# Gate products stacked in row groups, and the gate-up bias of an expert as four products of 32 rows

## The reference, cut to what matters

```
# in the mixer: a low-rank gate, rank 16, 1024 -> 16 -> 512
glr = xn @ w_in[:, glr columns]                        # 512 x 16
log_decay = log_sigmoid(glr @ gla_gate_up + gla_gate_bias) / 16
# in the experts: for every expert e and its (up to 128) rows
h = xb @ w_gate_up[e] + b_gate_up[e]                   # 128 x 2048
gate, up = min(h[:, ::2], 7), clip(h[:, 1::2], -7, 7)
act = (up + 1) * gate * sigmoid(1.702 * gate)
y = act @ w_down[e] + b_down[e]
```

## Time and profile before

| what | us |
|---|---|
| three runs: median (lowest, highest) | 1867.94 (1866.09, 1868.38) |
| the profiled execution: its own time | 1873.76 |
| span of its records | 1871.8 |
| PE, PEld busy | 1820.0 (97%), 1493.8 (80%) |
| DVE, ACT, POOL busy | 1402.6 (75%), 1112.8 (59%), 131.9 (7%) |
| experts stage, first product to the end | 708.2 to 1871.8 |

### The profile page before, as it was taken

The page is one execution under the profiler, slowest core; times in us unless marked ns, Lnnn a source line. Parts: engine busy times, 40 slices in busy tenths (PEclk is TensorE's granted clock), DMA queues, the critical chain, the costliest instruction groups (busy, mean ns, idle before and its releaser), DMA issues.

```text
span 1871.8 us, 24808 instructions
## 1 busy us (share of the span) xinstructions
PE 1820.0 (97%) x9054; PEld 1493.8 (80%) x9055; DVE 1402.6 (75%) x1294; ACT 1112.8 (59%) x994; POOL 131.9 (7%) x112
## 2 busy tenths in 40 slices
PE   6998999999999997999999999999999999999997
PEld 5776788898888875888888888888888888888885
DVE  3136444426333567999999999999999999999997
ACT  3343322226432254777777777777777777777774
POOL 0000100000000006000000000000000000000001
PEclk9998999999999997999999999999999999999998
DMA  6222042221233386999999999999999999999993
GB/s 210 72 85 67 23 170 90 90 68 36 91 113 121 118 305 228 369 376 369 367 376 365 363 379 368 368 379 368 364 382 367 373 374 368 372 375 372 368 376 127
DMA packets 100038, 493.56 MB, mean 264 GB/s; under 512 B 15434, under 2 KB 17482, under 8 KB 50320
## 3 DMA queue, kind: packets, MB, share of 16 engines
q1 hardware_dynamic: 90080, 475.63, 67.4%
q0 software_dynamic: 9616, 16.62, 3.5%
q10 hardware_dynamic: 288, 0.59, 0.1%
HBM read 484.57 MB, written 24.69 MB: 272 GB/s over the span
## 4 chain that ended last, share of the span: by engine, by line
PE 61%; DVE 1%; ACT 0%; POOL 0%; issue 0%; DVEq 0%; ACTq 0%
PE psum L1782 25%; PE psum L1785 12%; PE psum L1795 12%; PE psum L1800 6%; PE psum L1745 2%; PE psum L1753 1%; PE psum L1775 1%; DVE expert_chunk L1936 0%; DVE h_sb L2101 0%; DVE expert_lo L1626 0%; ACT expert_hi L1621 0%; POOL total_rstd L2019 0%; PE psum L1925 0%; PE psum L1919 0%; DVE gate_values L1865 0%; ACT up_values L2050 0%
## 5 line engine op out<-in xcount | busy, mean ns | idle before, releaser
L1626 DVE TENSOR_TENSOR expert_lo<-expert_chunk,expert_hi 128x2048 fp32r<-128x2048 f32 x384 | 864.5, 2285 | 46.3 <-ACT expert_hi L1621 37.3
L1621 ACT CAST expert_hi<-expert_chunk 128x2048 fp32r<-128x2048 f32 x384 | 735.4, 1917 | 233.7 <-PE psum L1785 201.6
L263 DVE TENSOR_TENSOR chunk_lo<-chunk,chunk_hi 128x2048 fp32r<-128x2048 f32 x48 | 109.9, 2290 | 283.1 <-ACT chunk_hi L259 283.0
L1782 PE MATMUL psum<-expert_hi,rowsT_hi 128*128 128x512 f32 x992 | 273.0, 397 | 0.0
L1782 PE MATMUL psum<-expert_hi,rowsT_lo 128*128 128x512 f32 x992 | 266.6, 391 | 0.0
L1785 PE MATMUL psum<-expert_lo,rowsT_hi 128*128 128x512 f32 x992 | 266.0, 390 | 0.0
L1782 PEld LDWEIGHTS psum<-expert_hi,rowsT_hi 128*128 128x128 f32 x992 | 182.2, 189 | 46.2 <-issue 11.6
L1782 PEld LDWEIGHTS psum<-expert_hi,rowsT_lo 128*128 128x128 f32 x992 | 186.8, 188 | 40.1
L1785 PEld LDWEIGHTS psum<-expert_lo,rowsT_hi 128*128 128x128 f32 x992 | 186.8, 188 | 38.9
L259 ACT CAST chunk_hi<-chunk 128x2048 fp32r<-128x2048 f32 x48 | 91.7, 1911 | 201.6 <-PE psum L294 174.4
L294 PE MATMUL psum<-chunk_hi,xT_hi 128*128 128x512 f32 x480 | 190.8, 398 | 5.2 <-DVE chunk_lo L263 3.6
(11 more groups left out here) (289 smaller groups left out, 1959.5 us busy)
## 6 DMA issues: line engine op xcount, KB each, us to landing
expert_chunk<-in_expert_w_gate_up SPq DMA_DIRECT2D x256, 1024.0 KB, 8.0
expert_chunk<-in_expert_w_down SPq DMA_DIRECT2D x128, 1024.0 KB, 6.8
chunk<-in_w_in SPq DMA_DIRECT2D x38, 1024.0 KB, 5.0
chunk<-in_w_branch_gla SPq DMA_DIRECT2D x4, 1024.0 KB, 5.1
chunk<-in_w_mix_out SPq DMA_DIRECT2D x4, 1024.0 KB, 5.1
gla_v<-in_x SPq DMA_DIRECT2D x4, 512.0 KB, 7.7
y_glaT_away<-h_sb SPq DMA_DIRECT2D x1, 2048.0 KB, 8.5
att_qT_then_y_glaT<-y_glaT_away SPq DMA_DIRECT2D x1, 2048.0 KB, 8.5
```

Source lines behind the costliest of these rows:

```text
L263: dve.tensor_tensor(self.wlo[c][:], self.raw[c][:], self.whi[c][:].bitcast(F32), ALU.subtract).then_inc(self.lo_done[c], 1)
L1621: act.copy(self.expert_hi[c % self.SLOTS][:], self.expert_ring[c % self.RING][:]).then_inc(self.moe["hi"], 1)
L1626: dve.tensor_tensor(self.expert_lo[s][:], self.expert_ring[c % self.RING][:], self.expert_hi[s][:].bitcast(F32), ALU.subtract).then_inc(se ...
L1782: pe.matmul(bank, x[:, k, :], whi[s][:, m // 2, m % 2 * COLS:(m % 2 + 1) * COLS], start=False, stop=False)
```

## The change

The diff has two parts; it has no line in the attention stage.

**Low-rank gate.** The 16 columns of the weights are written four times, 32 columns apart, as high, high, high, low, with zeros between (`w_lr_split`, a stationary operand of 128 x 128). Sixteen products (high and low part of x) fill all 128 rows of bank 4. ACT rounds the whole bank to `lrT`; DVE replaces rows 32 to 63 by their rest. The up weights are loaded four times, and split into high, high, low, high. `z` is then four float32r products with a contraction of 128 rows. POOL clears the two tiles first.

**Bias.** The table of gate-up biases is loaded once as 128 x 512, split, and stored to memory as `bias_table`. Per expert SP loads eight rows of 512 (four high, four low) so that rows 32m and 32m+1 of `bias_rows` hold the bias of bank m, all others being zero. The four products have a contraction of 32 rows each, with ones as stationary operand, in four different row groups. `pick_bias` goes.

```diff
-        w_lr_hi = self.sb(stack, "w_lr_hi", [P, KT, GLA_RANK], F32R)
-        w_lr_lo = self.sb(stack, "w_lr_lo", [P, KT, GLA_RANK], F32R)
+        w_lr_split = self.sb(stack, "w_lr_hi_hi_hi_lo", [P, KT, 4, QUARTER], F32R)
+        lrT = self.sb(stack, "lrT_hi_lo_hi_rest", [P, L], F32R)
+        up_split = self.sb(stack, "gate_up_hi_hi_lo_hi", [P, GLA_K_WIDTH], F32R)
...
+                sp.wait_ge(lr_cleared, 2)
+                for n in range(4):
+                    sp.dma_start(up[n * QUARTER:n * QUARTER + GLA_RANK, :], t["gla_gate_up"][0]).then_inc(up_in, 16)
...
+                pool.memset(up[:], 0.0).then_inc(lr_cleared, 1)
+                pool.memset(w_lr_split[:].bitcast(F32), 0.0).then_inc(lr_cleared, 1)
...
-                    for n, (w, xT) in enumerate(((w_lr_hi, self.x_hi), (w_lr_hi, self.x_lo), (w_lr_lo, self.x_hi))):
-                        last = pe.matmul(self.bank[4][0:GLA_RANK, :], w[:, k, :], xT[:, k, :], ...
+                    for n, xT in enumerate((self.x_hi, self.x_lo)):
+                        last = pe.matmul(self.bank[4], w_lr_split[:, k].rearrange("p g n -> p (g n)"), xT[:, k, :], ...
...
-                pe.wait_ge(small_in, 64)
-                pe.wait_ge(lr_out, 1)
+                pe.wait_ge(lr_rest, 1)
+                pe.wait_ge(up_lo, 1)
                 for h in range(H):
-                    pe.matmul(self.bank[4 + h], up[:, h * P:(h + 1) * P], lrT[:],
+                    pe.matmul(self.bank[4 + h], up_split[:, h * P:(h + 1) * P], lrT[:],
...
+                act.copy(w_lr_split[:, :, 0:3, 0:GLA_RANK], w_rank.unsqueeze(2).to_broadcast([P, KT, 3, GLA_RANK])).then_inc(lr_hi, 1)
...
-                act.copy(lrT[:], self.bank[4][0:GLA_RANK, :]).then_inc(lr_out, 1)
+                act.copy(lrT[:], self.bank[4]).then_inc(lr_out, 1)
+                act.wait_ge(up_in, 64)
+                act.copy(up_split[:], up[:]).then_inc(up_hi, 1)
...
+                    if g_ == base_r:
+                        dve.wait_ge(lr_out, 1)
+                        dve.tensor_tensor(lrT[part_rows(1), :], self.bank[4][part_rows(1), :],
+                                          lrT[part_rows(1), :].bitcast(F32), ALU.subtract).then_inc(lr_rest, 1)
+                        dve.wait_ge(up_hi, 1)
+                        dve.tensor_tensor(up_split[part_rows(2), :], up[part_rows(2), :], ...
...
-                for n in range(4):
-                    sp.dma_start(raw_bias[n * E:(n + 1) * E, :], t["expert_b_gate_up"][0]).then_inc(R["bias_in"], 16)
+                sp.dma_start(raw_bias, t["expert_b_gate_up"][0].rearrange("e (m n) -> (e m) n", n=COLS)).then_inc(R["bias_in"], 16)
...
-                sp.dma_start(self.bias_row[:], t["bias_row"]).then_inc(R["in"], 16)
...
-                sp.wait_ge(R["bias_lo"], 3)
+                sp.wait_ge(R["bias_lo"], 2)
+                sp.dma_start(self.bias_table.rearrange("e m s n -> (e m) s n"), bias[:].bitcast(F32)).then_inc(R["bias_stored"], 16)
                 for k in range(6, self.GU):
                     self.load_gate_up(sp, k, 0, k)
+                sp.wait_ge(R["bias_stored"], 16)
+                sp.wait_ge(R["rows_cleared"], 2)
+                for e in range(2):
+                    self.load_bias_rows(sp, e, e)
                 for b in range(NB):
                     sp.wait_ge(self.bank_free[b], last_mix + 1)
...
+                for rows in self.bias_rows:
+                    pool.memset(rows[:], 0.0).then_inc(R["rows_cleared"], 1)
...
-                for n in (1, 3):
-                    low_rows = slice(n * E, (n + 1) * E)
-                    dve.tensor_tensor(bias[low_rows, :], raw_bias[low_rows, :], bias[low_rows, :].bitcast(F32), ...
+                dve.tensor_tensor(bias[:, 1, :], raw_bias, bias[:, 0, :].bitcast(F32), ALU.subtract).then_inc(R["bias_lo"], 1)
...
+    def load_bias_rows(self, sp, e, u):
+        rows = self.bias_rows[u % 2]
+        for s in range(2):
+            sp.dma_start(rows[s:P:P // 4, :], self.bias_table[bass.ds(e, 1), :, s, :].rearrange("a m n -> (a m) n")
+                         ).then_inc(self.bias_in[u % 2], 16)
...
-        def gate_up_bias(pe, u):
+        def gate_up_bias(pe, e0, i=0):
+            pe.wait_ge(self.bias_in[e0 % 2], 32 * (i * self.UNROLL // 2) + 32 * (e0 // 2 + 1))
             for m, bank in enumerate(h_banks):
-                at = slice(m % 2 * 2 * E, (m % 2 + 1) * 2 * E)
-                pe.matmul(bank, self.pick[u][at, :], bias[at, m * COLS:(m + 1) * COLS], start=True, stop=False)
+                at = slice(m * (P // 4), (m + 1) * (P // 4))
+                pe.matmul(bank, self.ones[at, :], self.bias_rows[e0 % 2][at, :].bitcast(F32R), start=True, stop=False)
...
-                    pe.wait_ge(S["picked"], e + 2)
...
-                    if more:
-                        pick_bias(dve, e + 2, (e0 + 2) % self.UNROLL)
...
+                        if q == SLOTS and e0 < E - 2:
+                            self.load_bias_rows(sp, e + 2, e0)
```

More of the change, by code:

```diff
@@ L183, in build @@
                 with ExitStack() as moe:
-                    self.bias = self.sb(moe, "bias_hi_lo_twice", [P, 2 * self.WIDE], F32R)
+                    self.bias_split = self.sb(moe, "bias_hi_lo", [P, 2, COLS], F32R)
+                    self.bias_rows = [self.sb(moe, f"bias_rows{u}", [P, COLS]) for u in range(2)]
+                    self.bias_in = [self.sem(f"bias_rows_in{u}") for u in range(2)]
                     self.expert_hi = [self.sb(moe, f"expert_hi{j}", [P, 2, self.WIDE], F32R) for j in range(self.SLOTS)]
@@ L202, in build @@
                     self.lists = self.sb(moe, "lists_of_experts", [P, N_EXPERTS, 2])
-                    self.pick = [self.sb(moe, f"bias_pick{u}", [P, P], F32R) for u in range(self.UNROLL)]
+                    self.ones = self.sb(moe, "ones_r", [P, P], F32R)
                     self.index = [self.sb(moe, f"row_index{u}", [P, 1], I32) for u in range(self.UNROLL)]
@@ L614, in _ @@
                 act.wait_ge(lr_in, 16)
-                act.copy(w_lr_hi[:], w_rank).then_inc(lr_hi, 1)
+                act.wait_ge(lr_cleared, 2)
+                act.copy(w_lr_split[:, :, 0:3, 0:GLA_RANK], w_rank.unsqueeze(2).to_broadcast([P, KT, 3, GLA_RANK])).then_inc(lr_hi, 1)
                 self.run_groups("hi", act, base, GROUPS_QK, next_split=True,
@@ L711, in _ @@
                 dve.wait_ge(lr_hi, 1)
-                dve.tensor_tensor(w_lr_lo[:], w_rank, w_lr_hi[:].bitcast(F32), ALU.subtract).then_inc(lr_lo, 1)
+                dve.tensor_tensor(w_lr_split[:, :, 3, 0:GLA_RANK], w_rank, w_lr_split[:, :, 0, 0:GLA_RANK].bitcast(F32),
+                                  ALU.subtract).then_inc(lr_lo, 1)
                 for g_ in (base + 1, base_r, base_r + 1):
@@ L715, in _ @@
                         self.split_lo(dve, g_, c)
-                dve.wait_ge(small_in, 64)
+                    if g_ == base_r:
[3 more added lines that the diff above has]
+                        dve.wait_ge(up_hi, 1)
+                        dve.tensor_tensor(up_split[part_rows(2), :], up[part_rows(2), :],
+                                          up_split[part_rows(2), :].bitcast(F32), ALU.subtract).then_inc(up_lo, 1)
+                dve.wait_ge(small_in, 48)
                 for h in range(H):
@@ L1175, in mix_and_route @@
         raw_ones = self.sb(stack, "ones_sb", [P, P])
-        ones = self.sb(stack, "ones_r", [P, P], F32R)
+        ones = self.ones
         e_no = self.sb(stack, "expert_numbers_sb", [P, E])
@@ L1181, in mix_and_route @@
                                                  "powed", "hn_done", "turned", "hT_out", "scaled_w", "routed", "read", "low",
-                                                 "exps", "selected", "ranks", "pairs", "prepared", "empty")}
+                                                 "exps", "selected", "ranks", "pairs", "prepared", "empty", "rows_cleared",
+                                                 "bias_stored")}
         E_S = self.moe
-        bias, raw_bias = self.bias, self.expert_ring[7][:].rearrange("p k n -> p (k n)")
+        bias, raw_bias = self.bias_split, self.expert_ring[7][:, 0, 0:COLS]
         down_bias, raw_down = self.down_bias, self.expert_ring[6][0:3 * E, 0, :]
@@ L1380, in _ @@
                 self.split_hi(act, last_mix, 1)
-                act.wait_ge(R["bias_in"], 7 * 16)
-                act.copy(bias[:], raw_bias).then_inc(R["bias_hi"], 1)
+                act.wait_ge(R["bias_in"], 4 * 16)
+                act.copy(bias[:, 0, :], raw_bias).then_inc(R["bias_hi"], 1)
                 act.copy(down_bias[:], raw_down).then_inc(R["bias_hi"], 1)
@@ L1523, in _ @@
                 dve.wait_ge(R["bias_hi"], 2)
-                for n in (1, 3):
-                    low_rows = slice(n * E, (n + 1) * E)
-                    dve.tensor_tensor(bias[low_rows, :], raw_bias[low_rows, :], bias[low_rows, :].bitcast(F32),
-                                      ALU.subtract).then_inc(R["bias_lo"], 1)
```

(2 more changed lines are left out.)

28 lines of the change are left out of this document (12 added, 16 removed).

## The result

| | us |
|---|---|
| before, median of 4 runs | 1868.16 (1866.09 to 1869.14) |
| changed, median of 4 runs | 1852.87 (1852.45 to 1855.67) |
| ratio, 95% interval | 0.9918 (0.9905 to 0.9930) |
| changed, the profiled execution: own time; span | 1852.79; 1851.0 |

The changed kernel is 15.3 us faster; 1850.5 was forecast. Run again on another occasion it took 1853.54, ratio 0.9922 (0.9909 to 0.9935). The interval of the ratio is worth 13 to 18 us.

The account below looks back on a forecast made before the run. PE's dense product stream was taken as the bound. The bias was to save 11.0 us and the low-rank gate 6.4, together 17.4, giving a median of 1850.5 us, range 1846.5 to 1860.

Parts of the forecast that it names:

- What bounds it: Experts stage: PE's dense product stream sets the pace; DMA share is high only because chunks queue.
- Four at once: Bias block of each expert: four 32-row products start together in their own row groups and banks, saving 0.34 us.
- Rival (a): Bias products: four row groups but only two at a time; 11.0 us come back, 1861.5 us; chance 0.10.
- Thirty experts: 30 x 0.34: Bias blocks of experts 2 to 31 in the dense stream: 0.34 us saved each, 10.2 us in all.
- Experts 0 and 1: Bias blocks that start at the low clock: between 0.5 and 1.1 us saved, 0.8 taken.
- Low-rank products: Low-rank gate: 24 products in 5.56 us become sixteen in 3.6, saving 1.9 us.
- The clock behind z: Right behind z: the granted clock no longer falls to 0.50, saving 1.7 us; bounds 0 and 1.7.
- rival (b): Clock falls behind z all the same, 1852.2 us, or falls elsewhere, 1848.8 to 1854; chance 0.08 outside the forecast's 1848 to 1853.
- Costs set to nothing: Routing, gate and experts: dropped DVE and ACT work, added transfers, clears and new PE waits all priced at 0 us.
- rival (d): Routing: SP's wait for the stored bias table outlasts 693.28, delaying expert 0's gather; 5 us late gives 1855.5; chance 0.03.
- Rival (c): Dense experts: bias products bring the clock down, 1.7 us each, up to 51 us, 1901 us; chance 0.03.
- Rival (e): Bias block of each expert nearly free: 0.45 us saved each, 3.3 us more in all, 1847.2 us; chance 0.06.

Follow-up runs that it names:

- the kernel with 16 rows: Changed kernel with z made from the first 16 stacked rows alone in plain float32, other parts left out: 1858.70 us, ratio 0.9946 to the kernel before.

## Why the prediction was right, and which term was off

- **What bounds it: right.** PE's stream set the end. What came off it in the experts came off the time: 0.242 a period and 7.3 us for the bias alone.
- **Four at once: right.** The starts of the four lie within 0.01 us, and with two row groups in place of four the saving is gone. Rival (a) is out.
- **"Thirty experts: 30 x 0.34" is the term that was mis-sized.** A round is worth 0.24 us, so 7.3 us in place of 10.2. I took the distance between the starts of two pairs as what goes with a pair. It holds 0.11 us of the shape's fixed cost, and that stayed. My sentence "the change of shape before and behind them stays" was correct, and the working then took a part of it off. The row that should have warned me was in hand: the steps of a full stream are 0.226, and the earlier trace rows had 0.34, so the surplus needed a cause and a place after the change.
- **Experts 0 and 1: 0.8 forecast; not measurable.** The two profiles differ by 1.85 us between the bias of expert 0 and that of expert 2, but low clock takes 1.6 us less from the changed kernel's profile there, and the kernel with the gate part alone, which has the old bias products, needed only 69.73 us for the same stretch (72.33 before, 70.48 changed).
- **Low-rank products: 1.9 forecast, 1.83 measured. z: 2.8 forecast, 2.79 measured.** The weight loads of 188 ns stayed beside the products. That the load grew with the stationary's columns agrees with the Trainium skill, "TensorE: Matmul & The Clock Gate", section "LDWEIGHTS (loading the stationary operand)", in the slope only: 93 ns for 112 more columns are 0.83 ns each, as the page has it, but an estimate by its formula for the whole load is 13 ns for 16 columns and 107 for 128, where the traces have 95 and 188.
- **The clock behind z: 1.7 forecast, and the fall did go.** The reason (rows in use) was not borne out, see the kernel with 16 rows; that the term came true is luck. Its size isn't shown either: the gate part alone gave 7.0 us, of which 4.6 are products, and by the interval the rest is anything from 0 to 4.6. The profiles say that more went than the one stretch I priced: from 68 to 190 us the three with the old gate have 10.2 to 13.7 us of low clock, the nine with the whole new gate 0 to 6.8, six of them 3.4. The first half of rival (b), that the clock falls behind z anyway, is out. Its second half, that other falls move in or out, is what they do.
- **Costs set to nothing: held.** From the last router product to the first bias product there are 12.62 us in both profiles, so the work on DVE and ACT that went was worth nothing and SP's wait for the stored table cost nothing. The step ahead of the bias block is 0.32 us in all thirty dense experts, so PE's wait for the bias rows was always over. SP issues the last residual rows 2.3 us ahead of the last router product as before (681.58 and 683.89; 693.28 and 695.60 before), so rival (d) is out. DVE's split of the bias is one operation of 0.68 us, 0.69 forecast. PE has no idle time ahead of z, so its new waits there were over.
- **Rival (c), slower by a fall per expert: out.** The clock is 1.00 from 733.7 to 1839.6, over all thirty dense experts.
- **Rival (e), 0.45 each: out.** The fixed cost of the shape did not shrink.
- **The page's factor.** The prediction quoted the Trainium skill, "TensorE: Matmul & The Clock Gate", section "Measured speedup vs the span model", with 3.07 times for four row tiles, an estimated 0.29 us for the four. Measured: 0.44 to the next product and 0.64 for the block with its joints, in which a further four products cost 0.23 to 0.28. Four plain products take 0.93 here, so the gain of a single round is 0.93 over 0.64, 1.45 times. The factor doesn't hold for a single round between full products.

With 0.24 in place of 0.34 the sum would have been 17.4 - 2.9 = 14.5, and the forecast 1853.4, against 1852.87. That they meet within 0.6 us says little: the interval of the gain is 13 to 18 us, and the clock's share in it is not known.

## What to carry to other kernels

Price a block by the distance from the last product ahead of it to the second product behind it, less the plain steps in there, and not by the distance between two starts inside it: a start-to-start step can hold a cost that stays when the step goes. Row-tiled products between full ones pay a fixed 0.42 us here and then 0.23 to 0.28 per round, so they pay if several rounds stand together; a single round for four small products gains a third over leaving them full, and two half-filled rounds (0.87 in all) gain next to nothing. A look at the weight loads helps: where a load starts with its own product and not a step ahead, the step is longer than a plain one. When a clock stretch vanishes with an edit, count it only if several executions of either kind agree, and leave its cause open unless a kernel separates it.

## What the runs showed of the hardware

- The 32-row shape costs the same as the 64-row one: 0.66 us from the first of two rounds to the next full product in both.
- The fixed cost lies at three joints: 0.32 instead of 0.227 ahead of the block, 0.44 instead of 0.227 behind its first start, 0.34 instead of 0.227 behind the next product; together 0.41. Followed by transposes of 128 columns, the third is 0.165 instead of 0.109.
- At the first two joints the weight load starts with its own product (1012.72, 1013.16) and not 0.23 us ahead as in the plain stream. With four products of 128 rows in the same place there are no joints, and the loads start ahead.
- Float32 products of 128 rows were faster than of 16: z took 3.27 us against 3.94 from the product before to the one behind.
- How long the low clock lasts differs between executions of one kernel: the two profiles of the changed kernel have 45.5 and 52.3 us of it in their spans, and their own times differ by 2.8 (1852.79 and 1855.61).
- Between 137 and 150 us PE stands idle for 3.6 us in all 14 profiles, and in 13 of them the granted clock is at 0.50 from some moment between 140 and 150 us on, for 3.4 or 6.8 us. In the first profile of the changed kernel it stays at 1.00. Up to the last products every fall in the 14 profiles has an idle stretch of PE shortly ahead of it (1.4 to 4.0 us long), except those at or behind z with the old gate (98.2, 100.1 and 100.2): there PE was busy.
